# Masked products of the units with decay by channel: levels 0 and 1, 2 and 3, 4 and 5 issued and placed together

## The chip, the core and the metric

The kernel runs on one core of one Trainium2 chip. The core's engines are TensorE (PE: matmuls; PEld: its weight loads), VectorE (DVE), ScalarE (ACT), GpSimd (POOL) and SyncE (SP), which here only issues DMAs. Each engine runs its own instructions in the order in which they are written, and waits on semaphores for the others. The metric is the device time of one execution in microseconds; lower is better. A figure for a kernel is the median of its runs.

## What is computed

Two blocks on one sequence of 1024 tokens and 1024 channels. The first is a hybrid mixer (pooling and an mLSTM) and a mixture of experts. The second has two layers; each has four branches (HGRN2, retention, an SSD branch, GLA), then an output projection. The change is in the two branches whose state decays by channel, HGRN2 (4 heads of 128 channels) and GLA (4 heads of 64 channels):

```python
def chunked_vector_decay(q, k, v, log_f):
    def step(state, inp):
        qc, kc, vc, fc = inp
        cum = jnp.cumsum(fc, axis=-2)
        rel = jnp.where(causal, cum[..., :, None, :] - cum[..., None, :, :], -jnp.inf)
        scores = jnp.einsum('bhtd,bhsd,bhtsd->bhts', qc, kc, jnp.exp(rel))
        o = (jnp.einsum('bhts,bhsv->bhtv', scores, vc)
             + jnp.einsum('bhtd,bhdv->bhtv', qc * jnp.exp(cum), state))
        k_to_end = kc * jnp.exp(cum[..., -1:, :] - cum)
        state = (state * jnp.exp(cum[..., -1, :])[..., None]
                 + jnp.einsum('bhsd,bhsv->bhdv', k_to_end, vc))
        return state, o
```

## The kernel before

Everything is float32. Large products are made of three matmuls each (`mm3`, lines 136 to 138) on operands split into a rounded high part and a rest.

**Units.** A layer of the second block is worked through as 12 units, U = 0 to 11 in layer 0 and 12 to 23 in layer 1, of the kinds `KIND = "ssgghhhhrrrr"`. The kinds with decay by channel are g (GLA, units 2, 3, 14, 15; `count(U)` is 2, two heads of 64 channels) and h (HGRN2, units 4 to 7 and 16 to 19; one head of 128). A unit has a prep (its projections from the layer's input, its gates and running sums) and a core (its attention). While the core of unit U runs, the prep of U + 1 is woven in: `units` takes one step of the core on every engine, then as many steps of the prep as the list `PACE[U]` says. A prep step of PE is half a projection: 24 matmuls of 512 columns, or a quarter of the values' projection, 48 matmuls of 256 columns. `PACE` is worked out in `plan_units` from how many pieces of the work area WA are free.

**Levels.** In a core with decay by channel the scores of a chunk of 128 tokens are built by levels. Level l pairs the second half of every block of 2^(l+1) tokens with its first half, so that the decay between them can be split at the middle. For each level l:

- DVE or POOL writes the differences of the running sums into a tile `E, U, l`; ACT takes their exponential (L1936); DVE multiplies queries and keys in (`vector_factors`, L1945 and L1949, signal `fac`).
- PE makes the small products of queries and keys (L2030) for the eight chunks into one PSUM bank per head, under the name `pd`. Levels 0 to 5 use stationary tiles of 32 columns; level 6 uses 64.
- DVE copies the wanted entries into the score tile `P` with a mask (L2098, COPY_PREDICATED, signal `placed`), one instruction per head and level.

The core's steps are: a base product (L2010, placed by L2087); then levels 0 to 5, one in each step; then level 6 with the transposes of the keys to come (L1739, copied by ACT, L1746); the states (L1762, run up by DVE, L1774 and L1777); the outputs (L1796, L1804); and the norms (L1840, L1843, POOL L1852, ACT L1861). With level `ends_at(U)` DVE and ACT also make the factors to the chunk's end (L2104, L2059, L2109).

**What is woven between.** The prep of the next unit gives DVE the split of the next projection's weights (L1574, after ACT's L1569; PE waits for it as `w_lo` at the first half of that projection), the log-sigmoid steps (L2129, L2133), in layer 1 also the lower bound (L2237 to L2252), the running sum (L2255 or L4237), and the first two levels of the next unit (L1914, L1916). The unit before is finished by DVE in the second step of the core (`vector_finish`, L1892, L1896).

**Room.** `wa` (22 pieces of 1024 columns) and `banks` (the 8 PSUM banks) hand out the piece that has been free longest; who takes it waits for the signal with which the last user gave it back. A `pd` bank is given back by `placed`, the `E` tile of a level by PE's signal `prod`, a projection's bank by ACT's copy. Four banks (kind g) or two (kind h) hold a unit's outputs until the next unit's second step.

Of the kernel before, what the change touches and what calls it, by code (L numbers as in the profile page):

```python
# [160 lines left out]
def build(nc, d, out):  # L161
    ctx = ExitStack()
    with ctx:
# [53 lines left out]
        def ps(*key):  # L217
            return bank_aps[banks.has[key]]
# [5 lines left out]
        def brief(*key, end):  # L224

            banks.take(*key)
            banks.give(key, end)
# [1277 lines left out]
        def owner(U):  # L1505

            return U - U % 2 if KIND[U % 12] in "hr" else U
# [5 lines left out]
        def count(U):  # L1513
            return 2 if KIND[U % 12] == "g" else 1
# [213 lines left out]
        def plan_turn(U, src):  # L1728
            wa.take("KE", U)
            for i in range(2):  # L1730
                brief("turn", U, i, end=("turned", U, i))
            wa.give(src, ("turn", U, 1))
# [47 lines left out]
        def plan_outputs(U, n):  # L1780
            for i in range(2):
                banks.take("o", U, n, i)
            wa.give(("P", U, n), ("o_mm", U, n, 1))
            wa.take("osq", U, n)
            wa.take("orms", U, n)
# [35 lines left out]
        def late(U, n):  # L1821

            return U % 12 in (3, 4, 6, 10) and n == count(U) - 1

        def plan_norm(U, n):
            for i in range(2):
                brief("om", U, n, i, end=("oln", U, n, i))
            wa.give(("osq", U, n), ("om_mm", U, n, 1))
# [123 lines left out]
        def ends_at(U):  # L1952

            return 4 if U % 12 in (4, 5, 6) else 5

        def plan_decay(U):
            N = range(count(U))
            for n in N:
                wa.take("P", U, n)
                brief("base", U, n, end=("diag", U, n))  # L1960

            def products(l):
                for n in N:
                    brief("pd", U, l, n, end=("placed", U, l, n))
                wa.give(("E", U, l), ("prod", U, l, N[-1]))

            for l in range(6):
                if l < 5:
                    wa.take("E", U, l + 2)
                if l == ends_at(U):  # L1970
                    wa.take("F", U)
                    wa.take("E", U, 7)
                    wa.take("s", U)
                yield
                products(l)
            wa.give(("cum", U), ("fdif", U), ("decay", U, 7), ("end_decay", U))
            wa.give(("q", U), ("qfac_last", U))
            wa.give(("k", U), ("kfac_last", U))
            yield
            products(6)  # L1980
            plan_turn(U, ("F", U))
            yield
            for i in range(2):
                brief("kv", U, i, end=("state", U, 3 + 3 * i))
            wa.give(("KE", U), ("kv_mm", U, 1))
            yield
            for n in N:
                plan_outputs(U, n)
            wa.give(("E", U, 7), ("o_mm", U, N[-1], 1))
            wa.give(("s", U), ("o_mm", U, N[-1], 1))  # L1990
            if KIND[U % 12] == "g" or U % 2:
                for j in range(2):
                    wa.give(("v", owner(U), j), ("o_mm", U, N[-1], 1))
            for n in N:
                yield
                if not late(U, n):
                    plan_norm(U, n)

        def tensor_decay(t, U):
            N = range(count(U))  # L2000
            q, k = tl("q", U), tl("k", U)
            t.wait_ge(*at("copied", "q", U, 1))
            t.wait_ge(*at(*k_ready(U)))
            for n in N:
                free(t, banks, "base", U, n)
            for c in range(8):
                for n in N:
                    rows = head_rows(U, n)
                    for b in range(0, 128, 32):
                        o = t.matmul(ps("base", U, n)[b:b + 32, c * 32:(c + 1) * 32], c8(k)[rows, c, b:b + 32], c8(q)[rows, c, b:b + 32],  # L2010
                                     start=True, stop=True)
                    if c == 7:
                        o.then_inc(*up("scores", U, n, 0))

            def products(l):
                h = 1 << l
                E = tl("E", U, l)
                t.wait_ge(*at("fac", U, l))
                for n in N:
                    free(t, banks, "pd", U, l, n)  # L2020
                for c in range(8):
                    for n in N:
                        rows = head_rows(U, n)
                        chunk = c8(E)[rows, c, :]
                        keys = chunk if l else c8(k)[rows, c, :]
                        size, m = max(2 * h, 32), max(h, 32)
                        for b in range(0, 128, size):
                            second = chunk[:, b:b + size].rearrange("p (j b) -> p j b", b=2 * h)[:, :, h:2 * h]
                            to = ps("pd", U, l, n)[b:b + m, c * 64 + b // 2:c * 64 + (b + size) // 2]
                            o = t.matmul(to.rearrange("p (j r) -> p j r", r=h), keys[:, b:b + m], second, start=True, stop=True)  # L2030
                        if c == 7:
                            o.then_inc(*up("prod", U, l, n))

            for l in range(6):
                yield
                products(l)
            yield
            products(6)
            tensor_turn(t, U, tl("F", U), ("kfac_last", U))
            yield  # L2040
            tensor_states(t, U)
            yield
            t.wait_ge(*at("qfac_last", U))
            tensor_outputs(t, U, tl("E", U, 7), lambda n, i: ("placed", U, 6, n))
            for n in N:
                yield
                if not late(U, n):
                    tensor_norm(t, U, n)
# [29 lines left out]
        def vector_decay(v, U):  # L2078
            N = range(count(U))
            q, k, cum = tl("q", U), tl("k", U), tl("cum", U)  # L2080
            for n in N:
                free(v, wa, "P", U, n)
            squares = ident.rearrange("p (b t) -> p b t", t=32).unsqueeze(1).broadcast_to([128, 8, 4, 32])
            for n in N:
                scores = ps("base", U, n)[:, 0:256].rearrange("p (c t) -> p c t", t=32).unsqueeze(2).broadcast_to([128, 8, 4, 32])
                v.wait_ge(*at("scores", U, n, 0))
                v.tensor_tensor(tl("P", U, n).rearrange("p (c b t) -> p c b t", b=4, t=32), scores, squares, ALU.mult).then_inc(  # L2087
                    *up("diag", U, n))

            def products(l):  # L2090
                B, h = 2 << l, 1 << l
                for n in N:
                    pv = tl("P", U, n).rearrange("p (c j b) -> p c j b", c=8, b=B)[:, :, :, h:B]
                    mv = LM[:, l * 64:(l + 1) * 64].rearrange("p (j r) -> p j r", r=h).unsqueeze(1).broadcast_to([128, 8, 64 // h, h])
                    bv = ps("pd", U, l, n).rearrange("p (c j r) -> p c j r", c=8, r=h)
                    v.wait_ge(*at("prod", U, l, n))
                    v.wait_ge(*(at("placed", U, l - 1, n) if l else at("diag", U, n)))
                    v.copy_predicated(pv, mv, bv).then_inc(*up("placed", U, l, n))  # L2098

            for l in range(6):  # L2100
                vector_factors(v, U, l + 1)
                if l == ends_at(U):
                    free(v, wa, "F", U)
                    v.tensor_tensor(c8(tl("F", U)), c8(cum)[:, :, 127:128].broadcast_to([128, 8, 128]), c8(cum), ALU.subtract).then_inc(  # L2104
                        *up("fdif", U))
                yield
                products(l)
            v.wait_ge(*at("fdecay", U))
            v.tensor_tensor(tl("F", U), k, tl("F", U), ALU.mult).then_inc(*up("kfac_last", U))  # L2109
            v.wait_ge(*at("decay", U, 7))  # L2110
            v.tensor_tensor(tl("E", U, 7), q, tl("E", U, 7), ALU.mult).then_inc(*up("qfac_last", U))
            yield
            products(6)
            yield
            v.wait_ge(*at("end_decay", U))
            vector_states(v, U, lambda c: tl("s", U)[:, c:c + 1])
            yield
            yield from idle(len(N))
# [2863 lines left out]
```

## Time and profile before

| | |
|---|---|
| median of 3 runs | 3371.98 us (3370.20 to 3374.91) |
| the profiled execution | 3376.36 us |
| its span, first to last instruction | 3374.6 us |
| PE busy | 3327.1 us, 99% of the span, 23754 matmuls |
| DVE, ACT, POOL busy | 62%, 47%, 9% |
| granted TensorE clock | 0.993, on average |
| layer 0, units 2 to 7 | about 1640 to 2010 us from the span's start |
| layer 1, units 14 to 19 | about 2633 to 3006 us |

In the rows, times are in microseconds. A matmul of float32 operands stands in the trace as two records, so that a level has 64 in a unit of kind h (32 in level 5, 16 in level 6), and 128 in one of kind g. The end of a matmul is modelled, and matmuls overlap: what a matmul costs is read from the start of one to the start of the next, and not from its duration.

### The profile page before, as it was taken

What the parts mean: (1) busy time and instruction counts of PE and PEld (TensorE: products, weight loads), DVE (VectorE), ACT (ScalarE), POOL (GpSimd) and SP (SyncE); (2) the same over time, 40 slices, a digit from 0 to 9 for tenths busy, and PEclk for the clock granted to TensorE, in tenths of its full rate; (3) what the DMA queues carried; (4) which work ended last, traced back from release to release, by engine and by line L of the source; (5) the groups of instructions that cost most, each with busy time, mean ns of one, the idle gap of its engine ahead of it and who ended that gap; (6) DMA issues with size and microseconds to landing.
All of it is one profiled execution on the core that took longest, in us unless ns stands there. A gap on an engine that the chain in (4) does not pass through costs nothing. (4 is left out here: it accounts for less than half of the span.)

```text
span 3374.6 us, 55706 instructions
## 1 busy us (share of the span) xinstructions
PE 3327.1 (99%) x23754; PEld 2759.9 (82%) x23754; DVE 2100.3 (62%) x2531; ACT 1599.5 (47%) x1887; POOL 313.7 (9%) x265
## 2 busy tenths in 40 slices
PE   9999999999999998999999999999999999999998
PEld 7887776778888887888888888888788888888887
DVE  7655543469898887756656663455666567753544
ACT  5342111248888785443356543533443356643432
POOL 0000000001011102000123210000000123120000
PEclk9999999999999999999999999999999999999999
DMA  6211551369999997122111111243122111111433
GB/s 236 77 58 47 175 166 65 140 231 399 413 415 416 414 413 298 49 76 88 52 52 64 43 66 50 94 186 127 64 75 88 58 46 58 39 64 51 156 125 112
DMA packets 97245, 492.94 MB, mean 146 GB/s; under 512 B 10921, under 2 KB 11433, under 8 KB 59105
## 3 DMA queue, kind: packets, MB, share of 16 engines
q1 hardware_dynamic: 77216, 417.31, 32.4%
q0 software_dynamic: 14160, 51.55, 4.4%
q10 hardware_dynamic: 5616, 20.45, 1.5%
q8 instruction: 191, 3.13, 0.4%
q14 instruction: 62, 0.50, 0.0%
HBM read 431.43 MB, written 57.84 MB: 145 GB/s over the span
## 5 line engine op out<-in xcount | busy, mean ns | idle before, releaser
L136 PE MATMUL ps<-HH,WS 128*128 128x512 f32 (+1 forms) x2592 | 1034.6, 399 | 4.5 <-DVE WS L1574 2.7
L138 PE MATMUL ps<-HH,WS 128*128 128x512 f32 (+1 forms) x2592 | 1013.3, 391 | 0.1
L137 PE MATMUL ps<-HL,WS 128*128 128x512 f32 (+1 forms) x1952 | 762.3, 391 | 0.0
L136 PEld LDWEIGHTS ps<-HH,WS 128*128 128x128 f32 (+1 forms) x2592 | 487.2, 188 | 112.6 <-DVE WS L1574 6.4
L138 PEld LDWEIGHTS ps<-HH,WS 128*128 128x128 f32 (+1 forms) x2592 | 486.9, 188 | 106.9 <-issue 0.5
L1639 ACT ACTIVATE WA<-ps 128x512 f32<-128x512 f32 x240 | 142.9, 596 | 864.4 <-PE ps L138 841.9
L137 PEld LDWEIGHTS ps<-HL,WS 128*128 128x128 f32 (+1 forms) x1952 | 367.0, 188 | 74.7 <-issue 1.5
L136 PE MATMUL ps<-WAR 128*128 128x512 f32 x768 | 306.8, 399 | 0.9 <-DVE WAR L1368 0.9
L138 PE MATMUL ps<-WAR 128*128 128x512 f32 x768 | 301.0, 392 | 0.0
L1574 DVE TENSOR_TENSOR WS<-RAW,WS 128x1024 fp32r<-128x1024 f32 (+2 forms) x152 | 201.9, 1329 | 117.8 <-ACT WS L1569 117.8
L827 DVE TENSOR_TENSOR WRR<-WR,WAR 128x2048 fp32r<-128x2048 f32 x107 | 241.3, 2288 | 34.7 <-ACT WAR L823 34.7
L136 PE MATMUL ps<-WS,HH 128*128 128x256 f32 x896 | 257.8, 288 | 3.4 <-DVE WAR L2614 1.9
L137 PE MATMUL ps<-WS,HH 128*128 128x256 f32 x896 | 253.4, 283 | 0.0
L138 PE MATMUL ps<-WS,HL 128*128 128x256 f32 x832 | 235.4, 283 | 0.0
L823 ACT ACTIVATE WAR<-WR 128x2048 fp32r<-128x2048 f32 x107 | 200.3, 1917 | 11.7 <-ACT WA L954 8.9
L137 PE MATMUL ps<-HH,WS 128*128 128x512 f32 x512 | 199.2, 389 | 0.0
L2098 DVE COPY_PREDICATED WA<-LM,ps 128x512 f32<-128x512 int32 x112 | 97.7, 906 | 158.2 <-PE ps L2030 158.1
L1569 ACT ACTIVATE WS<-RAW 128x1024 fp32r<-128x1024 f32 (+2 forms) x152 | 170.2, 1120 | 32.1 <-PE ps L138 10.3
L136 PEld LDWEIGHTS ps<-WS,HH 128*128 128x128 f32 x896 | 171.6, 192 | 8.8 <-issue 7.4
L137 PEld LDWEIGHTS ps<-WS,HH 128*128 128x128 f32 x896 | 171.7, 192 | 0.4 <-issue 0.2
L4606 DVE TENSOR_TENSOR WS<-RAW,WS 128x1024 fp32r<-128x1024 f32 x64 | 78.3, 1224 | 149.1 <-ACT WS L4598 149.1
L138 PEld LDWEIGHTS ps<-WAR 128*128 128x128 f32 x768 | 144.8, 189 | 31.7
(416 smaller groups left out, 5310.3 us busy)
## 6 DMA issues: line engine op xcount, KB each, us to landing
WR<-in_weu SPq DMA_DIRECT2D x36, 1024.0 KB, 9.1
WR<-in_wed SPq DMA_DIRECT2D x36, 1024.0 KB, 9.0
WR<-in_weg SPq DMA_DIRECT2D x35, 1024.0 KB, 10.5
RAW<-in_wo SPq DMA_DIRECT2D x32, 1024.0 KB, 4.9
WA<-in_wada SPq DMA_DIRECT2D x48, 512.0 KB, 4.5
H<-in_weg SPq DMA_DIRECT2D x23, 1024.0 KB, 10.5
H<-in_weu SPq DMA_DIRECT2D x23, 1024.0 KB, 9.3
H<-in_wed SPq DMA_DIRECT2D x22, 1024.0 KB, 10.4
```

The lines of the kernel that those rows point to most:

```text
L136: t.matmul(o, l[0], r[0], start=st, stop=False)
L137: t.matmul(o, l[0], r[1], start=False, stop=False)
L138: return t.matmul(o, l[1], r[0], start=False, stop=sp)
L823: a.activation(rounded(j, p), raw_piece(*key), ACT.Copy).then_inc(*up("we_hi", j, p))
L827: v.tensor_tensor(rest_of(j, p), raw_piece(*part(j, p)), rounded(j, p).bitcast(F32), ALU.subtract).then_inc(*up("we_lo", j, p))
L1569: a.activation(parts(layer, n)[0], raw_of(layer, n), ACT.Copy).then_inc(*up("w_hi", layer, n))
L1574: v.tensor_tensor(lo, raw_of(layer, n), hi.bitcast(F32), ALU.subtract).then_inc(*up("w_lo", layer, n))
L1639: a.activation(half(tl(*dst), i), ps("pj", layer, n, i), func, scale=scale).then_inc(*up("copied", *dst, i))
L2098: v.copy_predicated(pv, mv, bv).then_inc(*up("placed", U, l, n))
L4606: v.tensor_tensor(lo, wo_raw(layer, i, k), hi.bitcast(F32), ALU.subtract).then_inc(*up("wo_lo", layer, i, k))
```

## The change

`products(l)`, PE's matmuls of a level and DVE's placing of it, is no longer called in every step from level 0 to 5, but for two levels at once in the steps of levels 1, 3 and 5. The same is written into the plan, so that banks and tiles are taken and given back in the new order. The number and the form of all instructions stay. The factors of a level (`vector_factors`) and the exponentials keep their step.

```diff
@@ plan_decay
                 yield
-                products(l)
+                if l % 2:
+                    products(l - 1)
+                    products(l)
@@ tensor_decay
             for l in range(6):
                 yield
-                products(l)
+                if l % 2:
+                    products(l - 1)
+                    products(l)
@@ vector_decay
                 yield
-                products(l)
+                if l % 2:
+                    products(l - 1)
+                    products(l)
```

`PACE` comes out the same for every unit, and the orders of ACT, POOL and SP are the same, instruction by instruction. On PE and DVE each even level stands one core step later. Where a prep step stood between levels 2k and 2k + 1 on PE, the two now form one run, and the two prep steps around the place that level 2k has left stand side by side. Runs of L2030 on PE, counted over the program: 76 before, 48 now. In units 4, 6, 16 and 18 no prep step stood between levels 1 and 2 or between 4 and 5; there the number of runs falls by 1, and in the other eight units by 3.

What follows are rows of the program's order: line, operation, what it writes and reads, form, and xcount. The new file has its lines up to six further down (L2032 is the old L2030, L2100 the old L2098, and so on).

PE at the start of unit 5's levels, and where level 1 stands, before:

```order
L1840 MATMUL ps<-WAR,OR 128x512 x2
L1843 MATMUL ps<-WAR,OR 128x512 x2
L2030 MATMUL ps<-WA 32x16 x32
L136 MATMUL ps<-WS,HH 128x256
...
L138 MATMUL ps<-WS,HL 128x256
L2030 MATMUL ps<-WA 32x16 x32
L136 MATMUL ps<-WS,HH 128x256
```

The same places now:

```order
L1840 MATMUL ps<-WAR,OR 128x512 x2
L1843 MATMUL ps<-WAR,OR 128x512 x2
L136 MATMUL ps<-WS,HH 128x256
...
L138 MATMUL ps<-WS,HL 128x256
L2032 MATMUL ps<-WA 32x16 x64
L136 MATMUL ps<-WS,HH 128x256
```

Level 0 has left its own place between the norm and the first prep step, and stands with level 1.

DVE in unit 16, from the factors of level 2 on, before:

```order
L2098 COPY_PREDICATED WA<-LM,ps 128x512
L1945 TENSOR_TENSOR WA<-WA 128x128x4
L1949 TENSOR_TENSOR WA<-WA 128x128x4
L1574 TENSOR_TENSOR WS<-RAW,WS 128x1024
L1892 SCALAR_TENSOR_TENSOR WA<-ps,PV,WA 128x512 x2
L1896 TENSOR_TENSOR WA<-WA 128x1024
L1892 SCALAR_TENSOR_TENSOR WA<-ps,PV,WA 128x512 x2
L1896 TENSOR_TENSOR WA<-WA 128x1024
L2098 COPY_PREDICATED WA<-LM,ps 128x256x2
L1945 TENSOR_TENSOR WA<-WA 128x64x8
L1949 TENSOR_TENSOR WA<-WA 128x64x8
L2098 COPY_PREDICATED WA<-LM,ps 128x128x4
```

and now:

```order
L1947 TENSOR_TENSOR WA<-WA 128x128x4
L1951 TENSOR_TENSOR WA<-WA 128x128x4
L1576 TENSOR_TENSOR WS<-RAW,WS 128x1024
L1894 SCALAR_TENSOR_TENSOR WA<-ps,PV,WA 128x512 x2
L1898 TENSOR_TENSOR WA<-WA 128x1024
L1894 SCALAR_TENSOR_TENSOR WA<-ps,PV,WA 128x512 x2
L1898 TENSOR_TENSOR WA<-WA 128x1024
L2100 COPY_PREDICATED WA<-LM,ps 128x512
L2100 COPY_PREDICATED WA<-LM,ps 128x256x2
L1947 TENSOR_TENSOR WA<-WA 128x64x8
L1951 TENSOR_TENSOR WA<-WA 128x64x8
```

The placing of level 0 stood ahead of the factors of level 2, the weight split and the finish of unit 15; now it stands behind them, next to level 1's.

## Rows read from the trace of the kernel before

**Rows 1.** The page, busy time and share of the span of PE.
```profile
PE 3327.1 (99%) x23754; PEld 2759.9 (82%) x23754; DVE 2100.3 (62%) x2531; ACT 1599.5 (47%) x1887; POOL 313.7 (9%) x265
```

**Rows 2.** Window, length; busy PE, PEld, DVE, ACT, POOL; clock, DMA share, GB/s.
```profile
2633.00:3006.00 373.00, 368.61 (x5267) 318.29 (x5266) 244.52 (x286) 207.12 (x256) 86.48 (x70) 1.00 0.15 54
```

**Rows 3.** Timeline of PE, unit 7: start, duration, instruction, count; projections of 512 columns.
```profile
1995.54 0.39 PE L138 MATMUL ps<-HH,WS 128*128 128x512 f32 x1
1995.86 0.74 PE L2030 MATMUL ps<-WA 128*32 128x16 f32 x64
1996.53 0.50 PE L136 MATMUL ps<-HH,WS 128*128 128x512 f32 x1
1996.86 0.39 PE L137 MATMUL ps<-HL,WS 128*128 128x512 f32 x1
...
2002.21 0.70 PE L2030 MATMUL ps<-WA 128*32 128x32 f32 x32
```

**Rows 4.** Timeline of PE, unit 7, projections of 256 columns.
```profile
1982.70 0.28 PE L138 MATMUL ps<-WS,HL 128*128 128x256 f32 x1
1982.91 0.74 PE L2030 MATMUL ps<-WA 128*32 128x16 f32 x64
1983.58 0.39 PE L136 MATMUL ps<-WS,HH 128*128 128x256 f32 x1
...
1989.52 0.73 PE L2030 MATMUL ps<-WA 128*32 128x16 f32 x64
```

**Rows 5.** Timeline of PE, unit 16, where levels 1 and 2 stand together.
```profile
2804.31 1.32 PE L2030 MATMUL ps<-WA 128*32 128x16 f32 x128
2805.56 0.50 PE L136 MATMUL ps<-HH,WS 128*128 128x512 f32 x1
```

**Rows 6.** Timeline of PE: unbroken stretches of 48 matmuls, of 512 and of 256 columns.
```profile
1618.93 0.47 PE L136 MATMUL ps<-HH,WS 128*128 128x512 f32 x1
...
1630.03 0.46 PE L2010 MATMUL ps<-WA 64*32 64x32 f32 x34
...
1963.84 0.28 PE L136 MATMUL ps<-WS,HH 128*128 128x256 f32 x1
...
1969.68 0.39 PE L2030 MATMUL ps<-WA 128*32 128x16 f32 x25
```

**Rows 7.** Timeline of PE, units 4 and 16; in brackets its idle time and who ended it.
```profile
1818.56 0.74 PE L2030 MATMUL ps<-WA 128*32 128x16 f32 x64 [0.25 <-DVE WA L1949]
...
2811.57 0.74 PE L2030 MATMUL ps<-WA 128*32 128x16 f32 x64 [0.23 <-DVE WA L1949]
...
2825.04 1.15 PE L2030 MATMUL ps<-WA 128*64 128x64 f32 x16 [0.17 <-DVE WA L1949]
...
2826.77 1.09 PE L1739 MATMUL ps<-CT,WA 128*128 128x128 f32 x8 [0.59 <-DVE WA L2109]
...
2835.09 1.80 PE L1762 MATMUL ps<-WA 128*128 128x128 f32 x14 [1.76 <-ACT WA L1746]
```

**Rows 8.** Timeline of DVE, unit 16.
```profile
2798.78 1.34 DVE L2098 COPY_PREDICATED WA<-LM,ps 128x512 f32<-128x512 int32 x1 [3.08 <-PE ps L2030]
...
2809.07 1.32 DVE L2098 COPY_PREDICATED WA<-LM,ps 128x512 f32<-128x512 int32 x1
...
2832.69 0.68 DVE L1916 TENSOR_TENSOR WA<-WA 128x512 f32<-128x512 f32 x1
```

**Rows 9.** Timeline of ACT, unit 16, where PE's L1762 waits for it.
```profile
2833.41 1.06 ACT L1936 ACTIVATE WA<-WA 128x1024 f32<-128x1024 f32 x1 [0.51 <-DVE WA L1916]
2834.37 1.07 ACT L1746 ACTIVATE WA<-ps 128x512 f32<-128x512 f32 x2
```

**Rows 10.** Timeline of DVE in unit 3, level 5: placing, then work up to the weight split.
```profile
1765.22 1.37 DVE L2098 COPY_PREDICATED WA<-LM,ps 128x512 f32<-128x512 int32 x2 [1.61 <-PE ps L2030]
...
1769.88 1.21 DVE L1574 TENSOR_TENSOR WS<-RAW,WS 128x1024 fp32r<-128x1024 f32 x1
```

**Rows 11.** Timeline of PE, the projection that waits for that split.
```profile
1772.75 0.47 PE L136 MATMUL ps<-HH,WS 128*128 128x512 f32 x1
```

## The prediction

> **What bounds the kernel now.** I read the page first: PE is busy 99% of the span [rows 1]. Then the busy time by window for the six changed units of layer 1: PE 368.6 of 373 us at a granted clock of 1.00, the higher of its two levels, DVE 244.5 us, ACT 207.1 us [rows 2]. So PE is the bound here, and time can be won only where PE issues more slowly than its work needs, or waits. The busy share hides the first, since matmuls overlap in the trace; the timeline of PE shows it, if one reads from start to start. The idle times in brackets in the same timeline show the second.
>
> **Removed: 28 changes between the projections and the small products.** First projections of 512 columns [rows 3]. The last L138 starts at 1995.54 and the first L2030 at 1995.86: 0.32 us, where a projection's matmul otherwise takes 11.10/48 = 0.23 us [rows 6]. That is 0.09 us too much on the way in. On the way out the first L136 takes 0.33 us (1996.53 to 1996.86): 0.10 us too much. A whole prep step between two levels lasts from 1996.53 to 2002.21, 5.68 us; two are 11.36 us. Without a level between them 48 such matmuls take 11.10 us (1618.93 to 1630.03), with one way in and one way out still in it [rows 6]. Side by side they save 0.26 us.
>
> The level itself: 64 records take 0.67 us up to the first L136 (1995.86 to 1996.53) [rows 3], and the 128 records of two levels that already stand together in unit 16 take 1.25 us (2804.31 to 2805.56) [rows 5]. The moved level adds 0.58 us to its new place and takes 0.67 us from the old: 0.09 us more. One merge between wide steps is worth 0.26 + 0.09 = 0.35 us.
>
> Narrow steps (256 columns): 5.94 us between two levels (1983.58 to 1989.52) [rows 4], 5.84 us where it follows a norm instead (1963.84 to 1969.68) [rows 6], so 0.10 us for the way out; the way in is 0.21 us (1982.70 to 1982.91) against 5.84/48 = 0.12 us, so 0.09 us. With the level's own 0.09 us: 0.28 us.
>
> The order gives 76 - 48 = 28 merges: 12 wide (levels 4 and 5 of units 2, 3, 5, 7, and the one merge of units 4 and 6, in each layer), 14 narrow, and 2 in units 2 and 14, where level 0 stands behind the float32 sums of the SSD branch. There the way out stays, so I take 0.18 us. Sum: 12 x 0.35 + 14 x 0.28 + 2 x 0.18 = 4.20 + 3.92 + 0.36 = **8.5 us**, all on the path, since PE has no other slack. Twelve of the 28 are in units of two heads, for which no row shows two levels together; the level's own 0.09 us may be 0 or twice as much there, so the bounds are 7.4 and 9.6 us.
>
> A rule bears on this. The small products use tiles of 128*32 or 64*32, the projections 128*128 [rows 3]. The Trainium skill ("TensorEngine Tiling (Array Packing)", Key Properties) says that changing the tiling mode, and not just the tile, drains TensorE. It gives no figure, and would have both costs go with the tile mode. The trace agrees that the change costs, but not that the mode explains it all: behind L4027, a full 128*128 product, the first L136 is as long (0.47 us) as behind L2030 (0.50 us) [rows 6, 3]. The sum takes the costs from the rows and needs no cause.
>
> **Removed: waits of PE in units 4 and 16.** PE waited 0.25 us for level 3's factors in unit 4; in unit 16 it waited 0.23 us for the same, 0.17 us for level 6's, 0.59 us for L2109 and 1.76 us for ACT's L1746 [rows 7], in all 3.0 us. Behind all of them is DVE. In unit 16 it stood idle 3.08 us until 2798.78 for level 0's product [rows 8], and from there on had no pause until 2833.4, where L1916 ends. It reached level 1's placing only at 2809.07 [rows 8], although PE had finished levels 1 and 2 by about 2805.6 [rows 5]. ACT's L1936 waited for L1916, and L1746, for which PE waits, is queued behind it [rows 9].
>
> Now DVE doesn't wait for level 0. It goes on at 2798.78 - 3.08 = 2795.70 with the factors of level 2, the split and the finish. These take 2809.07 - 2798.78 = 10.3 us with the placing of level 0 in it, 1.1 us; so DVE arrives at the pair at 2795.7 + 9.2 = 2804.9, about when PE has finished it (PE started levels 1 and 2 at 2804.31 [rows 5]; level 0's 0.67 us and its two changes, 0.19 us, ahead of the prep step are gone, so the pair runs from about 2803.4 to 2804.7). What follows took 2833.4 - 2809.1 = 24.3 us; with one more placing of 0.6 us it ends at 2829.8, and with a pause of up to 1 us for levels 2 and 3, at 2830.8. ACT then needs 2835.4 - 2833.4 = 2.0 us [rows 9]: ready at 2831.8 to 2832.8. PE without its waits and with one merge less arrives at 2835.1 - 1.8 - 1.0 - 0.35 = 2832.0. So the waits go, but for up to 0.8 us. I take the whole **3.0 us**, as the walk is nearer to that; the bounds are 0 (DVE falls behind elsewhere) and 3.4.
>
> **Added or moved.** Even levels are placed one step later. DVE's burst is four copies instead of two in a unit of two heads, but the first two run while PE makes the odd level. Nobody waits for `placed` but the next level on DVE, and those who take a bank over; the 8 banks go round, and a pair's bank is taken again after eight more, with two prep steps or more (11 us) between. Factors of every level are ready earlier or at the same point, since DVE doesn't stop at even levels. The E tiles of even levels are given back one step later; their takers then get other pieces, freed by units or stores that ended before. ACT, POOL and SP keep their order. I put all this at 0, under the cover of DVE's 128 us of free time in the window [rows 2]; one place is thin (first rival below).
>
> **Sum.** 3376.36 - 8.5 - 3.0 = 3364.9 us for the profiled execution. That one is 4.4 us above the median of the runs, so the median becomes 3371.98 - 11.5 = **3360.5 us**, 0.34% faster. About 0.2% (6.7 us, up to 3365.2) is what a measurement of this kernel tells from no change.
>
> **Rivals.**
>
> *The burst makes the weight split late (slower).* In unit 3 level 5's two copies start at 1765.22, the split ends at 1769.88 + 1.21 = 1771.09 [rows 10], and PE takes it at 1772.75 [rows 11]: 1.66 us to spare. There are ten such places, where a split stands behind an odd level's placing. At 0.65 us a copy the two more cost 1.3 us, less the 0.6 us in which PE still makes level 5: 0.7 us later, and it holds. But a copy can take 1.3 us [rows 8]. Four of those are 5.2 us, 3.8 us more than now, so that PE would wait 3.8 - 1.66 = 2.1 us ten times: 3371.98 - 11.5 + 21 = 3381.5 us. It decides from some 3.7 us a burst on. Against it: the slow copies stand where POOL and DVE both work, early in a unit, and the splits stand late. A milder form, with 3 to 10 us lost here or to banks, gives 3364 to 3371.
>
> The PSUM rule points the same way. The Trainium skill ("PSUM — Partial Sum Buffer", Summary: rules for kernel authors) says to evacuate promptly, as the memory is tight; this change places half the levels later. No run here shows whether it bites: none of PE's waits in the rows is for a placing [rows 7], but neither are two levels' banks held at once there, except for levels 1 and 2, or 4 and 5, of units 4, 6, 16 and 18.
>
> *DVE stays behind in unit 16.* Then only the merges count: 3371.98 - 8.5 = 3363.5 us. For it: the pause for levels 2 and 3 falls in the busiest stretch. Against: 3 us of idle time is moved ahead of it.
>
> *The merges don't bring what the rows say*, because the costs belong to a level's first matmul and its semaphore wait rather than to the change of kind. Then 0 to 3 us stay: about 3369.5. Rows 5 and 6 speak against it.
>
> *More is won*, as DVE running ahead removes small waits in other units: 3358.
>
> **How the numbers follow.** Forecast 0.55; DVE stays behind 0.17, of which 0.12 is beyond 0.2%; milder lateness 0.12; merges without gain 0.05; late splits 0.05, of which 0.04 slower by over 0.2%; more won 0.06. Faster: 0.55 + 0.12 + 0.06 = 0.73. Slower 0.04. Same 0.23. The range runs from 3357.5 (9.6 us of merges, 3.4 of waits, and 1.5 us for the spread of the medians) to 3368, which leaves out part of the milder lateness, the merges without gain and the late splits: about 0.17.
>
> **What would show it.** In the trace after: 48 runs of L2032; pairs of 1.25 us in one-head units; two wide prep steps side by side in about 11.1 us; PE's waits before L1762 and L1739 in unit 16 gone, and DVE without a pause ahead of the factors of level 2. The stretch of units 14 to 19 should be shorter by about 4.2 + 2.8 = 7 us, that of units 2 to 7 by 4.5 us. I am wrong if PE shows new idle time at the first L136 of a projection with DVE's split, or a placing, as releaser, or if a pair takes as long as two levels apart.

## The result, and the profile after

The changed kernel is slower: 3393.5 us (median of 6 runs, 3390.6 to 3398.4) against 3373.0 us beside it (3370.2 to 3376.2), a ratio of 1.0065 with a 95% interval of 1.0054 to 1.0075. The forecast was 3360.5 us, with a range up to 3368.0. The profiled execution took 3395.7 us, its span is 3393.9 us.

The page hides the loss. PE's row answers to [rows 1], and its busy time is the same to 0.5 us:

```profile
PE 3327.6 (98%) x23754; PEld 2765.5 (81%) x23754; DVE 2115.8 (62%) x2531; ACT 1599.2 (47%) x1887; POOL 329.3 (10%) x265
```

So I cut each layer at the first base product of a unit (L2010, now L2012), into the two units of two heads and the four of one head. Windows of the kernel after, in the columns of [rows 2]: layer 0, two heads and one head; layer 1, two heads and one head.

```profile
1625.13:1804.40 179.27, 170.61 (x2661) 149.32 (x2660) 92.65 (x111) 81.04 (x105) 33.34 (x27) 0.97 0.13 45
1804.40:2012.71 208.31, 207.28 (x2774) 180.45 (x2773) 148.69 (x163) 123.05 (x150) 63.25 (x46) 1.00 0.16 60
2627.60:2812.40 184.80, 173.37 (x2661) 151.25 (x2660) 97.29 (x116) 83.05 (x107) 33.34 (x27) 0.95 0.12 44
2812.40:3024.05 211.65, 208.24 (x2774) 180.45 (x2773) 161.60 (x178) 129.21 (x156) 63.28 (x46) 1.00 0.16 59
```

The same four of the kernel before, with as many matmuls in each:

```profile
1630.03:1797.70 167.67, 166.96 (x2661) 144.68 (x2660) 92.91 (x111) 81.22 (x105) 32.81 (x27) 1.00 0.13 48
1797.70:2008.50 210.80, 209.54 (x2773) 180.59 (x2773) 142.22 (x163) 123.15 (x150) 56.02 (x46) 1.00 0.16 59
2623.40:2790.70 167.30, 166.66 (x2661) 144.72 (x2660) 95.77 (x116) 83.24 (x107) 32.66 (x27) 1.00 0.14 48
2790.70:3004.70 214.00, 210.25 (x2773) 180.66 (x2772) 155.01 (x178) 129.12 (x156) 56.00 (x46) 1.00 0.16 58
```

With two heads the stretches are 11.6 and 17.5 us longer, 29 us in all; with one head 2.5 and 2.4 us shorter. PE has a gap between length and busy time of 8.7 and 11.4 us where it had 0.7, and the mean clock fell from 1.00 to 0.97 and 0.95. The 24.2 us of the four stretches less the 4.9 us by which the first base product came earlier (1625.1 for 1630.0) are the 19.3 us between the spans. Those 4.9 us aren't the change's, which begins behind this point: ahead of it the kernel before had 37.5 us at the lower clock and the kernel after 27.3. The medians differ by 20.5 us.

PE's waits name no engine for it. Columns: waited for, us in total, times, longest. The kernel before has no row of this kind:

```profile
PE ps L2032 <- issue: 15.0, 8, 2.7
PE ps L138 <- issue: 2.0, 1, 2.0
PE ps L136 <- issue: 1.8, 1, 1.8
```

"Issue" means that nothing in the profile held the engine. The timeline of PE shows where, here the pair of levels 2 and 3 of unit 14:

```profile
2667.77 0.39 PE L138 MATMUL ps<-HH,WS 128*128 128x512 f32 x1
2668.09 2.20 PE L2032 MATMUL ps<-WA 64*32 64x16 f32 x235
2672.76 0.38 PE L2032 MATMUL ps<-WA 64*32 64x16 f32 x21 [2.48 <-issue]
2673.07 0.79 PE L136 MATMUL ps<-HH,WS 128*128 128x512 f32 x1
2673.66 0.63 PE L137 MATMUL ps<-HL,WS 128*128 128x512 f32 x1
2674.09 0.63 PE L138 MATMUL ps<-HH,WS 128*128 128x512 f32 x1
...
2676.47 0.40 PE L138 MATMUL ps<-HH,WS 128*128 128x512 f32 x1
2676.70 0.40 PE L136 MATMUL ps<-HH,WS 128*128 128x512 f32 x1
```

The run breaks off after 235 of its 256 matmul records, inside a level and inside a head, where no semaphore stands, and goes on 2.5 us later. Behind it the projections come every 0.43 us instead of 0.23. That is the lower of the two clock levels, 1.2 GHz, as the window says:

```profile
2672.80:2676.20 3.40, 3.40 (x28) 2.71 (x29) 3.05 (x5) 0.00 (x0) 0.00 (x0) 0.50 0.02 5
```

The twelve pairs of two heads last, up to the next projection: 2.44, 4.42, 1.80, 4.45, 2.74 and 1.85 us in layer 0, 5.22, 4.98, 4.21, 3.53, 4.91 and 1.80 us in layer 1 (the third and sixth of each are levels 4 and 5, with 192 records instead of 256). One level took 1.19 us before, so 2.3 us were to be expected. Seven of them stop inside for more than 1 us; two more stops, of 2.1 and 2.4 us from start to start, fall on the first matmuls of the projection behind a pair. The nine are 20.5 us from start to start. The granted clock is at its lower level in eight stretches of 3.4 us within these units, in none before: seven begin within 1.5 us after a stop. The eighth (1628.3) stands behind the base product of unit 2, and PE had no idle time in the 5 us ahead of it; the same stretch is there in five of the other ten kernels, with pairs and without, so it isn't the change's. Behind the stops that end at 1670.1 and 1759.3 it stayed at 1.00.

**The sum closes.** The stops make 20.5 us. A stretch of 3.4 us at the lower clock costs 3.4 x (1 - 0.23/0.43) = 1.6 us, eight make 12.5 us (narrow projections lose a little less). Against them stand the 12 merges in units of two heads, 3.4 us by the prices forecast: 20.5 + 12.5 - 3.4 = 29.6 us; the windows say 29.1.

**What the packets say.** Of the kernel after, the page's row of the instruction queue (packets, MB, share), then, from the DMA view of 2669.8 to 2673.8, the bytes in 40 slices of 0.1 us and the only queue that moved anything:

```profile
q8 instruction: 191, 3.13, 0.4%
...
GB/s 0 0 0 164 0 0 0 0 0 0 0 0 0 0 0 0 0 0 0 0 0 0 0 0 0 0 0 0 0 0 0 0 0 0 0 0 0 0 0 0
...
q8 instruction: 1, 0.02, 1.8%
```

191 packets for 48546 records of PE (matmuls, weight loads, and those of its sequencer) are 254 records each, and 16 KB. The queue is PE's: wide_pairs below has 2560 records less and 181 packets, g_twice 5120 more and 211, that is one packet for each 256 records. In the run above one packet starts at 2670.1, just when PE stops, and PE goes on at 2672.76. The nine long stops stand after records 17315, 17827, 19875, 20643, 34723, 35491, 36003, 37283 and 38051 of PE: the differences are 512, 2048, 768, 14080, 768, 512, 1280 and 768, each a multiple of 256. Each time a packet had started 2.3 to 3.0 us before PE went on, and in seven of the nine it had started 0.8 to 1.2 us after PE had passed the place 256 records back (0.1 and 1.9 us in the others). From that place to going on are 3.2 to 4.3 us, once 2.4.

So the theory: PE's instructions come in packets of 256, the next one is asked for about 1 us after PE passes into the one before it, and PE stops where it gets through a packet in less than some 3.4 us. A projection needs 0.115 us for a record (matmul and weight load in 0.23 us), a packet of them 29 us. Small products of two heads need 1.19 us for 256 records (128 matmul records and 128 weight loads). A level alone, 256 instructions, has projections ahead and behind which fill up its packets; a pair of levels 0 to 3 has 512 in a row, which must take in a whole packet, and all eight of these pairs stop, six inside and two on the projection behind; a pair of levels 4 and 5 has 384, and one of four stops.

### The profile page after: what moved, and what is told of

Same layout as the page of the kernel before. It is cut to its first block and busy times, and to the rows that moved or that the text cites. A ratio compares the mean times of both kernels' runs of the same rounds, so it can differ in the third digit from the quotient of the medians.

```text
span 3393.9 us, 55706 instructions
## 1 busy us (share of the span) xinstructions
PE 3327.6 (98%) x23754; PEld 2765.5 (81%) x23754; DVE 2115.8 (62%) x2531; ACT 1599.2 (47%) x1887; POOL 329.3 (10%) x265
## 5 line engine op out<-in xcount | busy, mean ns | idle before, releaser
L1574 DVE TENSOR_TENSOR WS<-RAW,WS 128x1024 fp32r<-128x1024 f32 (+2 forms) x152 | 207.3, 1364 | 120.3 <-ACT WS L1569 120.2
L823 ACT ACTIVATE WAR<-WR 128x2048 fp32r<-128x2048 f32 x107 | 200.3, 1917 | 11.7 <-ACT WA L954 8.9
L1569 ACT ACTIVATE WS<-RAW 128x1024 fp32r<-128x1024 f32 (+2 forms) x152 | 170.2, 1120 | 32.9 <-PE ps L138 10.3
L136 PEld LDWEIGHTS ps<-WS,HH 128*128 128x128 f32 x896 | 175.2, 196 | 10.5 <-issue 9.4
L137 PEld LDWEIGHTS ps<-WS,HH 128*128 128x128 f32 x896 | 175.3, 196 | 0.9 <-issue 0.7
```

The source lines that it names most:

```text
L136: t.matmul(o, l[0], r[0], start=st, stop=False)
L137: t.matmul(o, l[0], r[1], start=False, stop=False)
L823: a.activation(rounded(j, p), raw_piece(*key), ACT.Copy).then_inc(*up("we_hi", j, p))
L1569: a.activation(parts(layer, n)[0], raw_of(layer, n), ACT.Copy).then_inc(*up("w_hi", layer, n))
L1574: v.tensor_tensor(lo, raw_of(layer, n), hi.bitcast(F32), ALU.subtract).then_inc(*up("w_lo", layer, n))
```

## The experiments

Theory S is this one. Theory B is that banks and placings hold PE up in units of two heads. Ratios are against the kernel before on the same chip (3371.1 us in the first four, 3371.2 us in the next four).

### 1. Pairs in the one-head units only (h_pairs)

```diff
@@ in the plan, on PE and on DVE, against the changed kernel
-                if l % 2:
-                    products(l - 1)
-                    products(l)
+                if count(U) == 1:
+                    if l % 2:
+                        products(l - 1)
+                        products(l)
+                else:
+                    products(l)
```

> Levels in pairs only in the one-head units (4 to 7, 16 to 19); the two-head units keep one level at a time. Theory S (supply): PE's instructions come in packets of 256, and PE stops where it gets through one packet faster than the next can be fetched; a pair of a two-head unit is a run of 512 instructions (256 matmuls, 256 weight loads), a pair of a one-head unit one of 256. Then nothing stalls here: no idle time of PE before L2032 with the releaser 'issue', no stretch at the lower clock in units 2 to 19, and 8 wide merges at 0.35 us and 8 narrow at 0.28 us make 5.0 us, with 0.65 us of small waits 5.7 us less than before (ratio 0.998). Theory B (banks and placings: two levels of two heads hold four banks and give DVE four copies, and PE waits for them) says the same of this kernel. Theory C (pairing as such costs, one-head units included): 5 us or more slower than before.

3367.4 us, ratio 0.9987 (0.9978 to 0.9996): faster by 3.7 us with 5.7 expected. No row with "issue" as releaser among PE's waits. The clock is 1.00 throughout in layer 0; in layer 1 one stretch at the lower clock stands behind the base product of unit 14 (2616.6), again without a stop, and the two-head units there are 1.5 us longer than before. Theory S had no such stretch. In the trace the one-head units are 2.3 and 2.35 us shorter, as in the changed kernel. Theory C falls.

### 2. Pairs in the two-head units only (g_pairs)

The same edit with `count(U) == 2`.

> Levels in pairs only in the two-head units (2, 3, 14, 15). Theories S and B: the whole loss is here, 20.5 + 5.7 = 26 us slower than before, with 7 to 11 stops of PE of 1.2 to 2.9 us and releaser 'issue'. Theory C: about half of the loss, 10 us.

3398.8 us, 1.0085 (1.0069 to 1.0100): 27.7 us slower. All of the loss is here. PE in unit 2:

```profile
1662.55 1.85 PE L2035 MATMUL ps<-WA 64*32 64x16 f32 x191
1666.21 0.84 PE L2035 MATMUL ps<-WA 64*32 64x16 f32 x65 [1.81 <-issue]
```

This kernel's times differ from those of the changed one, but not the places: the runs stop after records 191, 227, 180, 235, 185, 143 and 174, in both kernels. (At 143 the stop is only 0.7 us here; a longer one, 1.2 us, stands 256 records on, in the projection behind.) A wait for another engine would move with that engine.

### 3. The changed kernel with half as many small matmuls (wide_pairs)

```diff
-                        size, m = max(2 * h, 32), max(h, 32)
+                        least = 64 if len(N) == 2 and l < 5 else 32
+                        size, m = max(2 * h, least), max(h, least)
```

> The changed kernel, but in the two-head units the matmuls of levels 0 to 4 take 64 rows of keys and 32 columns instead of 32 and 16: the same sums and some entries beside them that the mask leaves out, in half as many instructions. A pair has 128 matmuls and 128 weight loads, 256 instructions; banks, waits, placings and order are those of the changed kernel. Theory S: the stops with releaser 'issue' are gone (under 1 us in all), no stretch at the lower clock in units 2 to 19; a level takes about 0.69 us as level 5 does with such counts, not 1.19 us, which saves 20 x 0.5 = 10 us; with the merges (8.5 us) and the small waits (0.65 us) 19 us less than before: 0.9943. Theory B: the stops stay, since no bank and no placing has moved: 20.5 - 10 = 10 us slower than before, 1.003.

3361.4 us, 0.9972 (0.9961 to 0.9983): 9.65 us less than before, and so 30 us less than the changed kernel. The stops inside the runs are gone and the clock is 1.00 from 2620 to 3010, with the same banks, waits and placings. This decides against theory B. A pair is whole:

```profile
2646.39 2.07 PE L2033 MATMUL ps<-WA 64*64 64x32 f32 x128
2648.38 0.50 PE L136 MATMUL ps<-HH,WS 128*128 128x512 f32 x1
```

The size was missed: 9.65 us for 19. A pair takes 2.00 us, not 1.4; a matmul of 64 rows and 32 columns goes at 15.6 ns a record, where I had taken the 10.8 ns of level 5's. In layer 1 the two-head units are 164.2 us long for 167.3 before: six merges at 0.3 us and ten levels at 0.13 us make 3.1. One stop of 1.3 us is left, on the projection behind the base product of unit 3 (1715.25), a place with 256 small instructions of its own.

### 4. Only the placings in pairs (dve_pairs)

```diff
@@ vector_decay alone
-                products(l)
+                if l % 2:
+                    products(l - 1)
+                    products(l)
```

> PE and the plan of banks as before, level by level; only DVE places two levels at a time, in the steps of levels 1, 3 and 5. Theory S: within 2 us of before, as PE's stream is the old one. Theory B (late placings hold PE up): 10 to 25 us slower, with idle time of PE before L2030 or L136 and DVE as releaser.

3376.6 us, 1.0017 (1.0008 to 1.0026): 5.5 us slower, more than theory S allowed and less than theory B. The reason is a bank: PE waits for a placing, 2.1 us each in units 4 and 16 and 0.6 us each in units 3 and 15, since in this kernel the plan still gives the bank away as if the even level had been placed in its old step. PE, and the clock behind the wait:

```profile
2804.23 1.32 PE L2030 MATMUL ps<-WA 128*32 128x16 f32 x128
2807.62 0.76 PE L136 MATMUL ps<-HH,WS 128*128 128x512 f32 x1 [2.07 <-DVE WA L2098]
...
2807.60:2810.80 3.20, 3.17 (x8) 2.52 (x9) 3.20 (x5) 3.15 (x4) 0.00 (x0) 0.50 0.25 100
```

The changed kernel has no wait of PE for a placing, so this is no part of its loss. But the row shows another thing: here PE stopped 2.1 us for DVE, and the clock fell behind it just so, in unit 16 and in unit 4. So a stop need not come from the packets to be followed by the lower clock. It isn't followed by it every time: PE's waits of 1.76 us for L1746, before and after, have a clock of 1.00 behind them. And the clock falls without a stop too, behind the base products of units 2 and 14.

### 5. The packets moved by half of one (page_shift)

```diff
@@ tensor_chunk_sum, ahead of the second block
-            for k in range(8):
+            for k in list(range(8)) * (2 if c < 4 else 1):
```

> The changed kernel with 32 matmuls of an earlier stage (the sum of squares ahead of the second block, chunks 0 to 3) issued twice, to the same values: 32 float32 matmuls are 64 matmul records and 64 weight loads, 128 instructions more ahead of unit 2, and nothing else is changed. Theory S (supply in packets of 256 instructions): every place at which a packet ends moves 64 matmul records ahead. In the changed kernel PE stopped after records 191, 227, 180, 235, 185, 143 and 174 of the runs of the pairs; now it stops after 127, 163, 116, 171, 121, 79 and 110, or one packet (128 records) later; the two stops that fell on records 9 and 2 of the projection behind a run come to stand in the run, after records 201 and 194. In all 10 stops or so and 17 to 21 us, as in the changed kernel. Theory B' (the stop belongs to a place of the program: a bank, a head, a chunk): the stops stay after 191, 227, 180, 235, 185, 143 and 174.

One run, 3412.1 us. Nine runs stop, for 20.2 us. Two of them:

```profile
1748.40 1.60 PE L2032 MATMUL ps<-WA 64*32 64x16 f32 x163
1752.04 0.96 PE L2032 MATMUL ps<-WA 64*32 64x16 f32 x93 [2.04 <-issue]
...
2683.80 1.66 PE L2032 MATMUL ps<-WA 64*32 64x16 f32 x171
2687.62 0.90 PE L2032 MATMUL ps<-WA 64*32 64x16 f32 x85 [2.16 <-issue]
```

227 became 163, 235 became 171, the two stops in projections came into the runs at 201 and 194; 191, 180, 143 and 174 became 255, 244, 207 and 238, that is 64 less and one packet on, the second of the two places named. Only 185 has no successor; instead the last pair of unit 15 stops, after 188. Nothing but the number of instructions ahead was changed, and all these stops again stand at multiples of 256 records, counted from the stops of the changed kernel, so this shows that the place is set by packets of 256, as theory S says. The time is above the changed kernel's for two reasons: the first base product stands at 1636.1 instead of 1625.1, of which the doubled matmuls are a part, and the four stretches are 3.9 us longer. With one run more can't be said.

### 6. The kernel before with doubled small matmuls (g_twice)

```diff
@@ tensor_decay, products: the matmul stands in a loop of its own
+                            for _ in range(2 if len(N) == 2 and l < 5 else 1):
```

> The kernel before, with every matmul of levels 0 to 4 of the two-head units issued twice, to the same place with the same values: 20 runs of one level with 256 matmul records (512 instructions) instead of 128. Order, banks, waits and placings are those of before. Theory S: most of the 20 runs stop for about 2 us with releaser 'issue', 40 us in all, and the clock is lower behind many of them; with 20 x 1.2 = 24 us for the matmuls themselves and some 1.4 us for each of 15 to 20 stretches at the lower clock the time is 80 to 95 us longer than before. Theory B (two levels' banks and placings at once): no stop, 24 us longer.

One run, 3472.2 us, 101 us more than before. All 20 runs stop, 17 of them inside and 3 on the first matmuls behind. PE's waits:

```profile
PE ps L2031 <- issue: 32.7, 18, 2.6
PE ps L136 <- issue: 2.1, 2, 1.3
PE ps L138 <- issue: 1.5, 1, 1.5
```

24 us are the matmuls, 36 us the stops by these rows (some 40 from start to start), and most of the rest the clock: in the two-head units it is at its lower level for 82 us, in stretches of 3.4 and 6.8 us, which at 1.6 us for each 3.4 are at most 38 us. Order, banks and placings are those of before, so neither pairing nor a bank is needed for the stops. Theory S had 80 to 95 us; the stretches at the lower clock were more than I had counted.

### 7. Three levels at a time in the one-head units (h_triples)

```diff
+                if count(U) == 1:
+                    if l % 3 == 2:
+                        products(l - 2)
+                        products(l - 1)
+                        products(l)
+                else:
+                    products(l)
```

> The one-head units take three levels at a time (0 to 2, 3 to 5; 192 and 160 matmul records, 384 and 320 instructions in a run), the two-head units one as before. Three banks are held at once, fewer than the four of a pair of two heads. Theory S: a run of 384 or 320 instructions takes in a whole packet of 256 in some cases only; by the places of the packets in the kernel before, 4 to 7 of the 16 runs stop, for 0.8 to 2 us each, 9 us in all, with about 1.4 us more each at the lower clock: some 16 us of loss against 24 merges at 0.3 us, 7.5 us; 5 to 12 us slower than before. Theory B: 7.5 us faster than before, no stop.

3378.9 us, 1.0028 (1.0018 to 1.0037): 7.8 us slower, inside the 5 to 12 us. Four of the eight runs of 384 instructions stop and one of the eight of 320 (two of these five stops fall in the projection behind), 10 us in all from start to start. Only one of the five has the lower clock behind it, where I had counted one each; two more stretches stand behind the base products of units 2 and 14. Unit 19:

```profile
2976.95 1.84 PE L2036 MATMUL ps<-WA 128*32 128x16 f32 x180
2980.95 0.30 PE L2036 MATMUL ps<-WA 128*32 128x16 f32 x12 [2.17 <-issue]
```

So units of one head stop too, once their runs have 320 or 384 instructions. What counts is the length of the run, not the number of heads.

### 8. The wider matmuls, one level at a time (wide_single)

The edit of wide_pairs, made to the kernel before.

> The kernel before (one level at a time) with the wider matmuls of wide_pairs in levels 0 to 4 of the two-head units. In wide_pairs a pair of 128 records takes 2.00 us, 1.00 us a level, against 1.19 us before, and the pair of levels 4 and 5 1.75 us against 1.19 + 0.69 - 0.08. Theory S: with no runs of over 256 instructions in before there is no stop to remove, so only 16 to 20 levels x 0.19 us = 3 to 4 us are won: 0.999. Then of the 9.65 us by which wide_pairs is faster, 6 to 7 us come from the pairs. Rival: wider matmuls are worth more than 0.19 us a level as the projections behind them start sooner, 0.9975 here, and the pairs bring nothing.

3372.2 us, 0.9999 (0.9990 to 1.0009). A level takes 1.06 us instead of 1.19, 2.6 us for twenty. The trace shows 1.4 us less in layer 1 and 2.5 us more in layer 0, where a stop of 1.1 us at the base product of unit 3 and two stretches at the lower clock stand. The 3 to 4 us expected don't show in the ratio, whose interval of 3 us either way they would just leave. Nearly all of wide_pairs' gain is therefore the pairs': 9.1 us between the two ratios, each uncertain by 3 to 4 us, with 8.5 us forecast for the merges.

### 9. POOL kept at work in unit 16 (pool_more)

This one is about the other term that failed, the waits of unit 16.

```diff
@@ gpsimd_decays, on top of wide_pairs
+            for i in range(8 if U == 16 and l == 6 else 0):
+                g.tensor_tensor(ev[:, :, 0:h], ref, cv[:, :, 0:h], ALU.subtract).then_inc(*up("again", U, i))
+                g.wait_ge(*at("again", U, i))
             g.tensor_tensor(ev[:, :, 0:h], ref, cv[:, :, 0:h], ALU.subtract).then_inc(*up("far_dif", U, l))
```

> wide_pairs with one change in unit 16: POOL issues the last of its ten operations there (line 1928, level 6) nine times instead of once, to the same values, so that it works some 9 us longer, until about 20 us after the unit's base product instead of 12. Theory P (DVE's and POOL's operations slow each other, and that is why DVE won only 0.96 us in unit 16 by not stopping at level 0): DVE's operations in that stretch, which took 0.67 to 0.73 us (L1945, L1949), 1.21 (L2136) and 1.21 (L1574) in wide_pairs, take 0.3 to 0.9 us longer each, DVE reaches L1916 3 to 5 us later, and PE's wait before L1762 in unit 16 grows from 1.8 to 5 to 7 us. Rival: DVE's durations stay as they were, the wait stays 1.8 us, and the time is that of wide_pairs, 10 us less than before.

One run, 3365.2 us, 6.6 us less than a run of the kernel before beside it (3371.9). First the changed kernel, DVE and POOL in unit 16. DVE goes on without a pause now, as forecast, but beside POOL:

```profile
2817.32 1.60 DVE L1945 TENSOR_TENSOR WA<-WA 128x512 f32<-128x512 f32 x1
...
2820.29 2.10 DVE L1574 TENSOR_TENSOR WS<-RAW,WS 128x1024 fp32r<-128x1024 f32 x1
...
2821.26 2.03 POOL L1928 TENSOR_TENSOR WA<-WA 128x512 f32<-128x512 f32 x1
```

The same L1574 took 1.22 us before, and the same L1928 1.04 us in DVE's pause. Now DVE with POOL idle, in wide_pairs:

```profile
2792.96 0.73 DVE L1945 TENSOR_TENSOR WA<-WA 128x512 f32<-128x512 f32 x1
...
2795.41 1.21 DVE L2136 SCALAR_TENSOR_TENSOR WA<-WA 128x1024 f32<-128x1024 f32 x1
```

and the same operations beside POOL's additional ones, up to the end of these:

```profile
2796.15 1.22 DVE L1948 TENSOR_TENSOR WA<-WA 128x512 f32<-128x512 f32 x1
...
2801.63 2.06 DVE L2139 SCALAR_TENSOR_TENSOR WA<-WA 128x1024 f32<-128x1024 f32 x1
2803.61 1.21 DVE L1574 TENSOR_TENSOR WS<-RAW,WS 128x1024 fp32r<-128x1024 f32 x1
...
2789.45 11.70 POOL L1929 TENSOR_TENSOR WA<-WA 128x512 f32<-128x512 f32 x8
2801.24 1.37 POOL L1931 TENSOR_TENSOR WA<-WA 128x512 f32<-128x512 f32 x1
```

0.73 became 1.22, 1.21 became 2.06, and with POOL's end at 2802.6 L1574 is back at 1.21. POOL's additional operations take 11.7 us, not 9. DVE reaches L1916 4.4 us later, and unit 16 is 4.4 us longer (53.2 for 48.8). Theory P holds for the durations, but not for the place of the wait: the wait before L1762 stays 1.7 us, and PE waits 3.0 us before small products for their factors and 1.4 us before L1739 instead. The Trainium skill ("SBUF — State Buffer", SBUF: two separate sides) says that DVE and GpSimd share a pair of ports which one operation holds to its end, and that on DVE's side this concerns, among others, operations with two inputs from SBUF. The trace agrees: the slower operations all read two tiles there, and L1892, which reads one of its two from PSUM, takes 1.40 us for two with POOL at work or idle (2822.31 after, 2803.78 before).

## Why the prediction was wrong

**The term that failed: "the level's own 0.09 us may be 0 or twice as much there, so the bounds are 7.4 and 9.6 us".** For the twelve merges in units of two heads I wrote that no row shows two levels together, and then bounded them by the rows of one-head units, in which a pair is a run of 256 instructions. In units of two heads it is one of 512. These merges brought 3.4 us by their forecast price and cost some 31: 20.5 of stops and 11 of the lower clock behind seven of them. The bounds should have covered what a run of 512 instructions does to PE's supply, and that term was put at nothing. No bound allowed an unseen form to cost instead of gain. The sentence "all on the path, since PE has no other slack" was right, and it is why the stops counted in full. Rows that could have warned stood in the page: the instruction queue with its 191 packets is there in the kernel before as well, and 256 records in 1.19 us are 25 times the rate of a projection.

The Trainium skill ("Runtime: NRT & Kernel Launch", Instruction fetch mechanics) says that instructions are refilled in blocks of 16 KiB, 256 instructions, and that crossing from one to the next is mostly hidden. The packets and the distances between stops agree with the block; stops of up to 2.9 us do not agree with the rest.

**The merges themselves were right.** There are 48 runs of L2032, a pair of one head takes 1.25 us, and two wide steps side by side 11.10 us, both as forecast. Answering to [rows 3, 5, 6], PE in unit 7:

```profile
1993.44 1.32 PE L2032 MATMUL ps<-WA 128*32 128x16 f32 x128
1994.70 0.50 PE L136 MATMUL ps<-HH,WS 128*128 128x512 f32 x1
...
2005.80 1.30 PE L2032 MATMUL ps<-WA 128*32 128x16 f32 x96
```

Where nothing stops PE, the price of 0.28 and 0.35 us holds to nine tenths: units 5, 6 and 7, in which no wait changed, are 1.95 us shorter for 2.17 forecast. All one-head units together are 4.8 us shorter, with the waits in it, for 5.0 of merges and 3.0 of waits.

**The waits: 3.0 us forecast, about 0.5 us came.** Unit 4's 0.25 us is gone, and unit 16's 0.23 us and 0.17 us for factors. But unit 16 as a whole is 0.95 us shorter, of which the merge is 0.35 us. Answering to [rows 7]:

```profile
2847.52 1.09 PE L1739 MATMUL ps<-CT,WA 128*128 128x128 f32 x8 [0.42 <-DVE WA L2115]
2855.84 1.35 PE L1762 MATMUL ps<-WA 128*128 128x128 f32 x10 [1.75 <-ACT WA L1746]
```

Unit 18 has a new one of 0.3 us before L1762, and is 0.4 us longer than before. The rival "DVE stays behind in unit 16" is what happened, to the size that it gave (only the merges count), by another road: not a pause for levels 2 and 3, of which there is none. Against the forecast walk DVE ends L1916 2.6 us late, counted from the unit's base product, and two steps of the walk make most of it.

The first is "these take 10.3 us with the placing of level 0 in it; so DVE arrives with 9.2 us". From the factors of level 2 to the pair DVE took 10.6 us (2817.32 to 2827.96), 1.4 us more, since the pause had been POOL's room. Here I carried the durations of a stretch in which DVE was idle into one in which it isn't.

The second is "with one more placing of 0.6 us". The first two placings took 2.5 us, where 1.1 + 0.6 had been counted, and POOL had ended before them (2826.3):

```profile
2827.96 2.75 DVE L2102 COPY_PREDICATED WA<-LM,ps 128x512 f32<-128x512 int32 x2
```

In the kernel before, POOL's last operation in unit 16 and DVE's copy of level 2:

```profile
2800.69 1.49 POOL L1928 TENSOR_TENSOR WA<-WA 128x512 f32<-128x512 f32 x1
...
2811.43 0.71 DVE L2098 COPY_PREDICATED WA<-LM,ps 128x512 f32<-128x512 int32 x1
```

The prediction says that the slow copies of [rows 8] "stand where POOL and DVE both work". That reading was wrong. Of the 112 copies of the kernel before, the 32 of levels 0 and 1 take 1.31 to 1.40 us each and the 80 of the other levels 0.69 to 0.76 us, and during 20 of the 32 POOL is idle. One of these is the second copy of [rows 8], at 2809.07: POOL had ended at 2802.2. What is slow is the copy of these two levels. That the pattern in which they write is the reason is likely, but no run varies it.

**The other rivals.** The weight splits are not late: PE's waits for L1574 are 2.7 us before and 2.8 after. No placing is waited for. The rival on the slow side gave 3381.5 us, by a mechanism that isn't there; its number is nearer by chance. The signs named for being wrong were new idle time with DVE as releaser "or if a pair takes as long as two levels apart": the second came, and more.

**Open.** Why a stop is followed by the lower clock in some places and not in others, and why the clock falls behind the base product of unit 2 or 14 in some executions without one. And whether the next packet could be asked for earlier.

## What to carry to other kernels

Joining short runs of small matmuls saves the changes between them only while the joined run stays short in instructions. Here runs of 256 had no stop over 1 us with one exception (the base product of unit 3, in four kernels), seven of 20 with 384 stopped, one of eight with 320, and every one of 512, 44 in all; some 3.4 us for 256 instructions is about the fastest at which PE was fed here. Count instructions of a run, weight loads included, and look for idle time with no releaser; if it stands inside a run, make the operations fewer and larger before making the run longer (wide_pairs, 0.9972 of the kernel before, is the fastest of all). And a pause of one engine may be the room in which another works: price what fills it at the durations found beside that other engine.

## What the runs showed of the hardware

- PE stops up to 2.9 us (3.5 us once, in page_shift) where a packet of 256 instructions is used up before the next has come; it goes on 2.3 to 3.0 us after that packet starts (2.2 to 3.2 us over all kernels). The place is fixed to the record, and moved by exactly 64 matmul records with 128 more instructions ahead.
- Behind seven of nine such stops, and behind two waits of 2.1 us for another engine, the granted clock was 0.50 for 3.4 us, which costs 1.6 us; behind the five stops of h_triples once. In g_pairs, page_shift and g_twice some of these stretches last 6.8 us. Without any idle time ahead, it was 0.50 for 3.4 us behind the base product of unit 2 in six of eleven kernels.
- Small matmuls of 64 rows and 32 columns go at 15.6 ns a record, those of 32 and 16 at 9.3 ns: half as many do the same work in 1.00 to 1.06 us instead of 1.19.
- DVE's operations with two tiles from SBUF take 1.2 to 1.5 us beside POOL's instead of 0.7, and 2.1 instead of 1.2; POOL's 1.5 to 2.0 instead of 1.0.
- Copies with a mask of 128x512 take 1.3 to 1.4 us in levels 0 and 1 and 0.7 us in the others, POOL at work or not.
